# Second attention: q and k of each head in a tile of their own, with the forget gates' sums beside them, and one score product of 128 partitions in place of two

## The reference

```python
def fox_attention(q, k, v, logf):
    # logit[t,s] = q_t.k_s/sqrt(hd) + F_t - F_s, F = cumsum(log f), causal softmax
    F = jnp.cumsum(logf, axis=-1)
    ...
        s = jnp.einsum('bhqd,bhkd->bhqk', qi, k) * scale
        s = s + Fi[..., None] - F[:, :, None, :]
        s = jnp.where(kpos[None, :] <= qpos[:, None], s, -jnp.inf)
        p = jax.nn.softmax(s, axis=-1)
        return jnp.einsum('bhqk,bhkd->bhqd', p, v)
```

## Time and profile before

| | |
|---|---|
| median of 3 runs | 2448.6 us (2448.44 to 2452.16) |
| profiled execution, whole | 2453.66 us |
| its span, first to last instruction | 2451.5 us |
| mean granted TensorE clock | 0.976 |
| PE busy | 2376.0 us, 97% of the span |
| PE weight loads busy | 1951.3 us, 80% |
| VectorE (DVE) busy | 969.7 us, 40% |
| ScalarE (ACT) busy | 879.7 us, 36% |
| GpSimd (POOL) busy | 1043.6 us, 43% |

### The profile page before, as it was taken

One profiled execution on the slowest core, in us unless ns is written; L12 is line 12 of the kernel. 1 busy time (PEld: TensorE's weight loads), 2 busy tenths in 40 slices (PEclk: granted clock), 3 DMA queues, 4 the chain that ended last, 5 costly groups with the idle time before them and its releaser, 6 DMA issues.

```text
span 2451.5 us, 33656 instructions
## 1 busy us (share of the span) xinstructions
PE 2376.0 (97%) x10912; PEld 1951.3 (80%) x10912; DVE 969.7 (40%) x1605; ACT 879.7 (36%) x1591; POOL 1043.6 (43%) x792
## 2 busy tenths in 40 slices
PE   9999999999999999999999999998999999999997
PEld 7888877888888888888888777776777788888886
DVE  6899994446505213100114144444343344110012
ACT  4235643233322323323333533334333343332331
POOL 3455653444444434444453433332112254544443
PEclk9999998999999999999999999999999999999998
DMA  4333442348638322333331233234111331333331
GB/s 149 95 98 108 142 167 61 89 149 278 239 103 281 101 86 82 96 97 95 98 95 53 85 105 99 88 96 142 39 39 40 120 96 50 102 96 97 97 94 60
DMA packets 129275, 263.91 MB, mean 108 GB/s; under 512 B 14208, under 2 KB 14336, under 8 KB 128544
## 3 DMA queue, kind: packets, MB, share of 16 engines
q1 hardware_dynamic: 119520, 236.51, 31.8%
q10 hardware_dynamic: 9664, 26.19, 2.8%
HBM read 250.02 MB, written 12.58 MB: 107 GB/s over the span
## 4 chain that ended last, share of the span: by engine, by line
PE 85%; DVE 9%; issue 3%; ACT 2%; POOL 1%; DMA 0%; ACTq 0%; DVEq 0%; POOLq 0%
PE bank L910 24%; PE bank L912 23%; PE bank L911 23%; PE bank L1223 2%; DVE bank L1514 2%; PE bank L1281 1%; PE bank L1138 1%; PE bank L1139 1%; PE bank L1140 1%; PE bank L1189 1%; PE bank L1019 1%; PE bank L1224 1%; DVE bank L1583 1%; PE bank L1269 1%; PE bank L1207 1%
## 5 line engine op out<-in xcount | busy, mean ns | idle before, releaser
L382 POOL TENSOR_TENSOR wlo<-raw,whi 128x512 fp32r<-128x512 f32 x750 | 993.7, 1331 | 1311.8 <-ACT whi L454 1311.3
L910 PE MATMUL bank<-a_hi,whi 128*128 128x512 f32 x1928 | 763.3, 396 | 9.5 <-DVE a_lo L1349 4.0
L454 ACT ACTIVATE whi<-raw 128x512 fp32r<-128x512 f32 x750 | 469.1, 627 | 813.6 <-PE bank L912 712.7
L912 PE MATMUL bank<-a_lo,whi 128*128 128x512 f32 x1928 | 753.7, 391 | 0.0
L911 PE MATMUL bank<-a_hi,wlo 128*128 128x512 f32 x1928 | 753.4, 391 | 0.0
L910 PEld LDWEIGHTS bank<-a_hi,whi 128*128 128x128 f32 x1928 | 363.3, 188 | 95.8 <-issue 9.9
L912 PEld LDWEIGHTS bank<-a_lo,whi 128*128 128x128 f32 x1928 | 363.6, 189 | 77.1
L911 PEld LDWEIGHTS bank<-a_hi,wlo 128*128 128x128 f32 x1928 | 363.6, 189 | 72.6
L910 PE MATMUL bank<-b_hi,whi 128*128 128x512 f32 x852 | 336.2, 395 | 0.6 <-DVE b_lo L1652 0.3
L911 PE MATMUL bank<-b_hi,wlo 128*128 128x512 f32 x852 | 332.9, 391 | 0.0
L912 PE MATMUL bank<-b_lo,whi 128*128 128x512 f32 x852 | 332.9, 391 | 0.0
(11 more groups left out here) (243 smaller groups left out, 1939.7 us busy)
## 6 DMA issues: line engine op xcount, KB each, us to landing
raw<-d_stream SPq DMA_DIRECT2D x750, 256.0 KB, 2.6
G<-d_ada SPq DMA_DIRECT2D x72, 512.0 KB, 4.5
spill_rv<-tmp ACTq DMA_DIRECT2D x32, 256.0 KB, 2.1
G<-spill_rv ACTq DMA_DIRECT2D x6, 1024.0 KB, 10.3
G<-d_x ACTq DMA_DIRECT2D x4, 512.0 KB, 5.8
spill_ga<-sq ACTq DMA_DIRECT2D x8, 256.0 KB, 3.6
G<-spill_ga ACTq DMA_DIRECT2D x1, 2048.0 KB, 8.1
G<-d_x ACTq DMA_DIRECT2D x1, 2048.0 KB, 13.4
```

Of the source, the lines that this page charges most:

```text
L382: pool.tensor_tensor(wlo[:, s % SRING, :], raw[:, s % RING, :], whi[:, s % SRING, :].bitcast(F32), ALU.subtract).then_inc(lo_done, 1)
L454: act.activation(whi[:, p % SRING, :], raw[:, p % RING, :], ACT.Copy).then_inc(hi_done, 1)
L910: pe.matmul(out_ps, w_hi, hi[:, k, :], start=first and q == 0, stop=False)
L912: mm = pe.matmul(out_ps, w_hi, lo[:, k, :], start=False, stop=last and q == len(ks) - 1)
```

## The change

Each head gets tiles of 128 partitions for q and for k, in two pairs (`QH`, `KH`; pair h // 2 % 2). Even heads have q and k on partitions 0 to 63, the forget sums (in k) and ones (in q) on 64 to 95, zeros on 96 to 127. Odd heads have q and k on 64 to 127, the sums and ones on 32 to 63, zeros on 0 to 31. The scores are then one float32 matmul of 128 partitions. For this,
- `keep_qk` copies each half (64 partitions) to its head's tile: two ScalarE instructions instead of one;
- `beside_heads` writes ones and zeros, six VectorE memsets of 32x512 per pair: for pair 0 after the first attention, for pair 1, which lies where r was, after the products with Silu;
- `forget_sums` writes into the k tile (float32) and waits on scores three heads back instead of one; the sums are needed on two sets of partitions, so there are two more DMAs after L747 and VectorE waits for all three;
- the cast of the ones goes, and the mask columns are made for both sets of partitions (two small VectorE instructions instead of one);
- the tiles of the gates and of the `pa` projection lie in other places.

```diff
-        QF = tiles(8 * T, 4)
-        FHL, FLO, NFH, ONES_R = b_lo[:, 9, :], b_lo[32:48, 10, :], b_hi[:, 8:10, :], b_lo[:, 8, 0:P]
-        GA2, PA7 = tiles(12 * T, KD), tiles(B0 + 4 * T, 7)
+        FHL, FLO = b_lo[:, 9, :], b_lo[32:48, 10, :]
+        GA2, GB2 = tiles(12 * T, KD), tiles(B0, KD)
+        QH = [tiles(8 * T, 4)[:, 0:2, :], tiles(B0 + 4 * T, 4)[:, 0:2, :]]
+        KH = [tiles(8 * T, 4)[:, 2:4, :], tiles(B0 + 4 * T, 4)[:, 2:4, :]]
+        ROWS, FROWS = [slice(0, 64), slice(64, 128)], [slice(64, 96), slice(32, 64)]
...
             act.dma_start(FHL[48:64, :].bitcast(F32), FLO.bitcast(F32)).then_inc(ld_f, 16)
+            act.dma_start(FHL[64:80, :].bitcast(F32), FHL[32:48, :].bitcast(F32)).then_inc(ld_f, 16)
+            act.dma_start(FHL[80:96, :].bitcast(F32), FLO.bitcast(F32)).then_inc(ld_f, 16)
...
             def keep_qk(j):
                 wait_used(act, "qkb", 0, 2 * j + 1)
-                act.activation(QF[:, j % 4, :], bank_of("qkb", j)[:, :], ACT.Copy,
-                               scale=FOX_HD ** -0.5 if j % 2 == 0 else 1.0).then_inc(evac_of("qkb", j), 1)
+                to = (KH if j % 2 else QH)[j // 2 % 2]
+                for e in range(2):
+                    ins = act.activation(to[ROWS[e], e, :], bank_of("qkb", j)[ROWS[e], :], ACT.Copy,
+                                         scale=1.0 if j % 2 else FOX_HD ** -0.5)
+                ins.then_inc(evac_of("qkb", j), 1)
...
-                pe.matmul(s_ps, QF[r, at, t * P:(t + 1) * P], QF[r, at + 1, 0:n], start=True, stop=False)
-                pe.matmul(s_ps, ONES_R[32:64, :], NFH[32:64, h % 2, 0:n], start=False, stop=True)\
-                  .then_inc(fox_s, 1)
+                pe.matmul(s_ps, q[:, t * P:(t + 1) * P], k[:, 0:n], start=True, stop=True).then_inc(fox_s, 1)
...
-            own.next(dve.tensor_copy(ONES_R, ones[:, :]))
-            own.next(dve.tensor_tensor(small[32:64, 7, :], ident[32:64, 32:48], ident[32:64, 48:64], ALU.add))
+            for e in range(2):
+                at = FROWS[e].start
+                own.next(dve.tensor_tensor(small[FROWS[e], 7, :], ident[FROWS[e], at:at + 16], ident[FROWS[e], at + 16:at + 32],
+                                           ALU.add))
...
             def forget_sums(h):
-                if h >= 2:
-                    dve.wait_ge(fox_s, 4 * (h - 1))
-                dve.tensor_scalar(NFH[32:64, h % 2, :], FHL[32:64, :].bitcast(F32),
-                                  small[32:64, 7, h:h + 1], None, ALU.mult).then_inc(fox_nf, 1)
+                if h >= 4:
+                    dve.wait_ge(fox_s, 4 * (h - 3))
+                rows = FROWS[h % 2]
+                dve.tensor_scalar(KH[h // 2 % 2][rows, h % 2, :], FHL[rows, :].bitcast(F32),
+                                  small[rows, 7, h:h + 1], None, ALU.mult).then_inc(fox_nf, 1)
+            def beside_heads(pair):
+                q, k = QH[pair], KH[pair]
+                for e in range(2):
+                    empty = slice(96, 128) if e == 0 else slice(0, 32)
+                    dve.memset(q[FROWS[e], e, :], 1.0)
+                    dve.memset(q[empty, e, :], 0.0)
+                    dve.memset(k[empty, e, :], 0.0)
...
-            dve.wait_ge(ld_f, 16)
+            beside_heads(0)
+            dve.wait_ge(ld_f, 48)
             forget_sums(0)
...
+            dve.wait_ge(r_prod, 2 * GLA_HEADS)
+            beside_heads(1)
             maximum(0)
             maximum(1)
```

More of the change, by code:

```diff
@@ L199, in build @@
         OB = G[:, 0:8 * T].rearrange("p (n t) -> p n t", t=D)
-        QF = tiles(8 * T, 4)
         PR, PT = tiles(B0, 2), tiles(B0 + 2 * T, 2)
-        FHL, FLO, NFH, ONES_R = b_lo[:, 9, :], b_lo[32:48, 10, :], b_hi[:, 8:10, :], b_lo[:, 8, 0:P]
-        GA2, PA7 = tiles(12 * T, KD), tiles(B0 + 4 * T, 7)
+        FHL, FLO = b_lo[:, 9, :], b_lo[32:48, 10, :]
[3 more added lines that the diff above has]
+        ROWS, FROWS = [slice(0, 64), slice(64, 128)], [slice(64, 96), slice(32, 64)]
         def gb2(m):
-            return QF[:, m, :] if m < 4 else tiles(B0, 4)[:, m - 4, :]
+            return GB2[:, (m + 4) % 8, :]
         def pa_out(m):
-            return PA7[:, m, :] if m < 7 else sq[:, 0, :]
+            return tiles(B0 + 8 * T, 3)[:, m, :] if m < 3 else tiles(8 * T, 4)[:, m - 3, :] if m < 7 else sq[:, 0, :]
         assert B0 + 11 * T <= G_END and 20 * T <= X0
@@ L867, in _ @@
             act.dma_start(GA2[:, :, :], spill_rv[:, 2 * KD:3 * KD, :]).then_inc(ld_ga, 16)
-            act.dma_start(QF[:, :, :], spill_rv[:, 3 * KD:3 * KD + 4, :]).then_inc(ld_gb, 16)
-            act.dma_start(tiles(B0, 4), spill_rv[:, 3 * KD + 4:4 * KD, :]).then_inc(ld_gb, 16)
+            act.dma_start(GB2[:, 4:8, :], spill_rv[:, 3 * KD:3 * KD + 4, :]).then_inc(ld_gb, 16)
+            act.dma_start(GB2[:, 0:4, :], spill_rv[:, 3 * KD + 4:4 * KD, :]).then_inc(ld_gb, 16)
             for m in range(KD):
@@ L1213, in scores @@
                 n = (t + 1) * P
-                r = slice(FOX_HD * (h % 2), FOX_HD * (h % 2 + 1))
-                at = h // 2 % 2 * 2
+                q, k = QH[h // 2 % 2][:, h % 2, :], KH[h // 2 % 2][:, h % 2, :]
                 s_ps = bank[6 + u % 2][:, 0:n]
```

## The result

The changed kernel took 2411.73 us in the median of 4 runs (2409.68 to 2413.24), the kernel before 2450.27 us in 4 runs beside it. The ratio is 0.9844, 95% interval 0.983 to 0.9857: 38.5 us faster. The forecast was 2412.4 us, a gain of 36.2. The profiled execution took 2411.95 us, its span 2409.8, against 2453.66 and 2451.5. The median of 2448.6 us from which the forecast counts is of three runs; the ratio uses the four.

The account below looks back on a forecast made before the run. PE, busy all 60.00 us in mid-loop, was taken as the bound. 41.0 - 1.2 - 1.3 - 2.3 = 36.2 us off the 2448.6 us median gave 2412.4 us, range 2404 to 2430.

Parts of the forecast that it names:

- The product itself: Loop scores: one 128-row float32 product replaces two and the shape changes go, saving 2.56 us a head, 41.0 over 16.
- the load rule quoted from the Trainium skill: Weight loads overlap matmuls only on different row groups; 128-row loads would wait, gain 21.8 us; rival 2429.7 us, chance 0.10.
- The deductions: Three parts of the saving not reaching the end: units 0 and 1, last four heads, stretch ahead of the loop; -1.2, -1.3, -2.3 us.
- The hidden savings of units 0 and 1: Their scores precede PE's wait at L1253, so savings of 0.56 and 0.61 us only lengthen it: -1.2 us.
- the copy bites: Last four heads, fourth query block: PE waits for ScalarE's copy L854, saving 0.19 instead of 0.61; three units, -1.3 us.
- The stage: Ahead of the loop: memsets 2.9, halved copy before Silu 0.6, less 1.2 absorbed waits; loop 2.3 us later (bounds 0, 3.5).
- the rival of a spell ahead of the loop: A second or longer low-clock spell ahead of the loop: 6.8 us more, 2419.2 us; chance 0.15.
- the one of the vanishing spell: The low-clock spell vanishes or falls into VectorE's waits, where it costs nothing: 2405.6 us; chance 0.08.
- The clock: Around the loop's start 13.6 us run at the lower clock, 6.8 lost; taken as unchanged, 6.8 us either way as bound.
- the forecast's unit of 2.7 us: Sign expected in the profile after: a loop unit of 3.32 - 0.64 = 2.7 us.
- Edits costed at nothing: First six memsets, 14 other split copies, forget rows, two DMAs, gate loads: no cost; uncovered, memsets 2.9 and copies 8.3 us.

Follow-up runs that it names:

- rows64: The changed kernel with its score product on the 64 rows of q and k alone, forget sums left out; 2430.26 us, ratio 0.9927 to the kernel before.
- no_second: The kernel before without its second score product (L1224), the 64-row product left as it is; 2432.95 us, ratio 0.9936.
- second128: The changed kernel with a second 128-row product (zeros times forget sums, split type) added to each unit's scores; 2418.39 us, ratio 0.9882.
- spread_fill: The changed kernel with the second pair's six memsets moved into the loop, two each at units 1, 2 and 3; 2408.09 us, run again 2407.43.
- spread_warm: The changed kernel with those memsets spread over units 1 to 3 and PE's wait ahead of the transposes filled with 20 matmuls of ones; 2408.83 us.
- before_split: The kernel before with each copy of q and k from PSUM (L814) made as two copies of 64x512; 2451.30 us, ratio 1.0006.

## Why the prediction was right

**The product itself** was the right term for the right reason, and an eighth too small. The forecast had 2.56 us per head; 2.92 were there by the pieces, 2.90 by the distance from head to head. The streaming of the new product came as said (L1230 to L919 grows by 0.20 to 0.23 for each 128 keys; L1195's pace gives 0.21), and the entry and the two load waits of 0.20 went. What was missed is a fourth piece of 0.09 per unit. Behind a return to 128 rows the next product is late once more: L910 to L911 is 0.33 us in the earlier trace rows's units (1760.45 to 1760.78), and only 0.23 between later pairs. I had read to the start of L910 and stopped. That the price belongs to the shape is shown by rows64 and no_second (a 64-row product alone still costs 0.39 us more per unit) and by second128 (another 128-row product doesn't). second128, where every tile is 128x128, also shows what the load rule quoted from the Trainium skill (TensorE: Matmul & The Clock Gate, What overlaps and what doesn't) would forbid: loads on the same rows beside a product in flight, without a wait (the added product costs 0.16 us for 384 keys, its columns alone). The trace disagrees with that rule here.

**The deductions.** The hidden savings of units 0 and 1 stand as argued; no run tested them alone. PE's wait there was to grow by 1.8 us and grew by 0.96, since the scores stand behind the halved copy as Silu does. A deduction is missing: the scores issued in unit 0 save nothing either, because PE waits 1.42 us for the copy L862 behind them. The forecast took the 0.72 us of the earlier trace rows for PE's wait; that row is the weight load's, and PE's own row there shows none. In the last four heads the copy bites as said. The changed kernel there:

```profile
...
1868.56 0.97 PEld L1286 LDWEIGHTS bank<-G 128*128 128x128 f32 x8 [0.65 <-ACT G L862]
...
1881.38 0.61 PE L1274 MATMUL bank<-consts,G 128*128 128x128 f32 x4
...
1881.82 0.60 PE L1230 MATMUL bank<-G 128*128 128x256 f32 x2
1882.02 0.60 ACT L862 ACTIVATE G<-bank 128x512 f32<-128x512 f32 x1 [2.28 <-PE bank L1274]
...
1882.67 0.97 PEld L1286 LDWEIGHTS bank<-G 128*128 128x128 f32 x8 [0.65 <-ACT G L862]
...
```

The kernel before, two heads apart:

```profile
...
1869.62 0.49 PE L1223 MATMUL bank<-G 64*128 64x128 f32 x2
...
1902.54 0.49 PE L1223 MATMUL bank<-G 64*128 64x128 f32 x2
...
```

The copy ends at 1882.62, and the product with v starts at 1882.67. A head lasts 14.11 us there (1868.56 to 1882.67), and lasted 16.46 (1869.62 to 1902.54 for two), so it saves 2.35 and not 2.92. The unit with the wait saves 0.18; the forecast had 0.19.

**The stage** was undersized: 2.3 us predicted; the loop starts 4.5 us later, of which 0.3 were there already where VectorE leaves the first attention (the first memset at 1675.3, against L1822 at 1675.0). Of 4.2 us the halved copy ahead of Silu makes 0.7 (0.6 forecast), the memsets 1.9 (stage 16.4 to 14.5 in spread_fill; 2.9 less 1.2 = 1.7 forecast), and 1.6 go with the low clock in the stage, which vanish in spread_warm. The first two were priced right. The third is the rival of a spell ahead of the loop, at a quarter of its 6.8 us, and it came true in the same execution as the one of the vanishing spell.

**The clock** was taken as unchanged. In the profiled pair it was not: 13.6 us at the lower level left the loop and 3.4 us went into the stage; in the 170 us after the loop 13.6 us instead of 10.2 lay at the lower level, and the part after the loop took 511.6 us instead of 509.8. In the sum of the spans: loop -48.0 (of which up to 6.8 clock), start of the loop +4.5, after the loop +1.8, together -41.7. But that is this pair. Over the runs the clock cost both kernels the same, 53 to 55 us (see Experiments), so the 38.5 us between the medians are not the clock's. For the time "unchanged" came out right, but not because the spell stayed in its place. That the one execution kept for the kernel before was 3.4 us above its median fits this: its mean granted clock is 0.976, and 0.978 is the mean of the others.

**The sum again.** At full clock the loop of the kernel before takes 229.9 us or more; before_split, whose spell is only 3.4 us, gives 231.2. Against 188.7 that is 41.2 to 42.5 us, where the forecast had 38.5 (41.0 - 1.2 - 1.3). The stage costs 2.6 us apart from the clock, where it had 2.3. So 38.6 to 39.9 us by the traces, 38.5 by the medians and 36.2 forecast: the product was too small by 0.36 us per head, 5.7 in all; the missing deduction in unit 0 (0.7), larger ones in the last heads and at units 0 and 1 (0.6 together) and the stage (0.3) took back 1.6, and some 1 to 2 us more aren't located. That these errors point opposite ways, and the time came within 2.3 us, is luck. So is the forecast's unit of 2.7 us, which fits a head of 10.84 us: its 3.32 us were the mean of three units that leave out the longest, and a head of 13.74 us makes 3.44.

**Edits costed at nothing.** The copies in the loop cost nothing there (before_split). The first six memsets, the two DMAs and the forget sums were not tested alone; no wait of the changed kernel's trace names them, and the 0.3 us above is all that is seen ahead of them.

## What to carry to other kernels

Read a product's price by the distance between starts, up to the second matmul behind it, and split it into a part that grows with columns and one that doesn't. A part that doesn't grow next to tiles of another shape is, in this kernel, the price of a change of shape; pad the small product to the shape of its neighbours, or fold its rows into the empty rows of another. Instructions that only prepare a later use belong where their engine idles, and in small portions, since six in a row held PE for 0.9 us here.

## What the runs showed of the hardware

- A change of the number of rows from one product to the next cost PE 0.10 us on the way from 128 to 64 rows, 0.20 each from 64 to 32, from 32 to 128 and from 64 to 128, and 0.09 more behind the return to 128. Both ways back to 128 cost the same, from float32 (64 rows) and from the split type (32 rows), and between tiles of 128 rows the passage from float32 to the split type costs nothing (second128). The Trainium skill (TensorEngine Tiling (Array Packing), Key Properties) says that changing the tiling mode drains the engine; the trace agrees in that these costs stand only beside such a change, and the prices are the trace's.
- The lengths of these instructions don't depend on rows: a memset of 32x512 takes 485 ns like one of 128x512, a copy of 64x512 0.59 us like one of 128x512. The memsets of the changed kernel:

```profile
...
L1839 DVE MEMSET G<- 32x512 f32 x4 | 1.9, 485 | 0.8 <-DVE small L1821 0.3 <-DVE G L1864 0.2
...
```

- The low-clock spell at the loop's start was 13.6 us in two profiled executions with 64-row scores, 3.4 us in three and absent in one; in the seven profiled executions with 128-row scores, two of them of the changed kernel, it never came. Filling the wait ahead of it did nothing. Each is one execution, and a 64-row kernel was without it too; whether the shape of the scores keeps it away, and how, is open.
- Executions differ before the changed part as well: Silu starts between 1680.5 and 1689.5 us, with 65 to 79 us at the lower clock ahead of the stage. For effects of 1 to 3 us the distances within the trace said more than the totals.
